# Weight columns interleaved by stage, reversed operands in four stages, and 256 bytes behind the split weight tiles

## The reference, cut to what matters

```python
z = modulate(rmsnorm(x, norm1_g), shift1, scale1) @ w_in + b_in          # stage w_in
x = x + gate1 * (concat(rmsnorm(y_a), rmsnorm(y_b)) @ w_out)             # stage w_out
g_ff, up_ff = split(h2 @ w_ffn_in, 2)                                    # stage ffi0
x = x + gate2 * ((silu(g_ff) * up_ff) @ w_ffn_out)                       # stage ffo0
```

## Time and profile before

| | us |
|---|---|
| median of 2 runs | 1760.57 (1760.45 to 1760.68) |
| profiled execution, first to last instruction | 1757.1 |
| around the span (median less span) | 3.5 |
| PE busy in the span | 1679.6 |
| PEld (weight loads) busy | 1311.8 |
| VectorE busy | 916.1 |
| ScalarE busy | 627.2 |
| GpSimd busy | 225.3 |

### The profile page before, as it was taken

One profiled execution on the slowest core, in us unless ns is written; L12 is line 12 of the kernel. 1 busy time (PEld: TensorE's weight loads), 2 busy tenths in 40 slices (PEclk: granted clock), 3 DMA queues, 4 the chain that ended last, 5 costly groups with the idle time before them and its releaser, 6 DMA issues.

```text
span 1757.1 us, 22185 instructions
## 1 busy us (share of the span) xinstructions
PE 1679.6 (96%) x8263; PEld 1311.8 (75%) x8263; DVE 916.1 (52%) x1376; ACT 627.2 (36%) x946; POOL 225.3 (13%) x204
## 2 busy tenths in 40 slices
PE   1999899999999999999999999999998999999996
PEld 1757688888888867666667788888887688888885
DVE  6765676544334463666667544444336644444223
ACT  1324334222223362554555333333226333333221
POOL 5010106998000030000000000003000000000000
PEclk9999999999999999999998999999999899999998
DMA  7565134454332241111101322233211133333221
GB/s 281 204 200 167 40 110 161 169 181 157 109 107 97 69 117 64 37 37 49 37 25 61 108 96 95 95 100 115 98 57 49 61 98 100 99 96 115 92 80 48
DMA packets 48588, 179.27 MB, mean 102 GB/s; under 512 B 5968, under 2 KB 6640, under 8 KB 48272
## 3 DMA queue, kind: packets, MB, share of 16 engines
q1 hardware_dynamic: 43600, 162.04, 27.5%
q0 software_dynamic: 3776, 14.78, 2.7%
q10 hardware_dynamic: 1152, 1.66, 0.4%
HBM read 173.04 MB, written 2.10 MB: 100 GB/s over the span
## 4 chain that ended last, share of the span: by engine, by line
PE 71%; issue 22%; DVE 5%; DMA 1%; ACT 1%; ACTq 1%; POOL 0%; POOLq 0%; DVEq 0%; SPq 0%
PE bank L383 15%; PE bank L385 14%; PE bank L384 14%; PE bank L1437 3%; PE bank L1439 2%; PE bank L1438 2%; PE bank L1545 2%; PE bank L1501 2%; PE bank L1521 2%; DVE ada_acc L1972 1%; PE bank L1172 1%; PE bank L1174 1%; PE bank L1173 1%; PE bank L454 1%; PE bank L1394 1%
## 5 line engine op out<-in xcount | busy, mean ns | idle before, releaser
L309 DVE TENSOR_TENSOR w_lo<-raw,w_hi 128x1024 fp32r<-128x1024 f32 (+1 forms) x229 | 316.4, 1382 | 575.2 <-ACT w_hi L305 574.9
L305 ACT ACTIVATE w_hi<-raw 128x1024 fp32r<-128x1024 f32 (+1 forms) x229 | 258.0, 1127 | 564.4 <-PE bank L385 482.7
L383 PE MATMUL bank<-h_hi,w_hi 128*128 128x512 f32 x1136 | 448.0, 394 | 0.5 <-DVE w_lo L309 0.5
L385 PE MATMUL bank<-h_hi,w_lo 128*128 128x512 f32 x1136 | 442.2, 389 | 0.0
L384 PE MATMUL bank<-h_lo,w_hi 128*128 128x512 f32 x1136 | 442.2, 389 | 0.0
L383 PEld LDWEIGHTS bank<-h_hi,w_hi 128*128 128x128 f32 x1136 | 213.2, 188 | 50.2 <-issue 5.2
L385 PEld LDWEIGHTS bank<-h_hi,w_lo 128*128 128x128 f32 x1136 | 213.2, 188 | 45.0
L384 PEld LDWEIGHTS bank<-h_lo,w_hi 128*128 128x128 f32 x1136 | 213.3, 188 | 44.6 <-issue 1.7
L383 PE MATMUL bank<-hid_hi,w_hi 128*128 128x512 f32 x528 | 205.6, 389 | 0.0
L384 PE MATMUL bank<-hid_lo,w_hi 128*128 128x512 f32 x528 | 205.4, 389 | 0.0
L385 PE MATMUL bank<-hid_hi,w_lo 128*128 128x512 f32 x528 | 205.4, 389 | 0.0
(11 more groups left out here) (397 smaller groups left out, 2079.5 us busy)
## 6 DMA issues: line engine op xcount, KB each, us to landing
raw<-in_f2i SPq DMA_DIRECT2D x88, 512.0 KB, 3.3
raw<-in_ffi SPq DMA_DIRECT2D x44, 512.0 KB, 3.4
raw<-in_f2o SPq DMA_DIRECT2D x32, 704.0 KB, 4.0
ada_w<-in_ada_w SPq DMA_DIRECT2D x24, 512.0 KB, 4.3
m_out<-in_ada_w POOLq DMA_DIRECT2D x24, 512.0 KB, 3.7
raw<-in_att_w SPq DMA_DIRECT2D x23, 512.0 KB, 3.3
raw<-in_ffo SPq DMA_DIRECT2D x16, 704.0 KB, 4.0
raw<-in_ada_w SPq DMA_DIRECT2D x16, 512.0 KB, 4.9
```

Source lines behind the costliest of these rows:

```text
L305: nc.scalar.activation(WH[par][:, 0:kc * P], RAW[s][:, 0:kc * P], ACT.Copy).then_inc(whi, count)
L309: nc.vector.tensor_tensor(WL[par][:, 0:kc * P], RAW[s][:, 0:kc * P], WH[par][:, 0:kc * P].bitcast(F32), ALU.subtract).then_inc(wlo, count)
L383: pe_.matmul(bank[:, :], w_h, hi[:, k0 + k, :], start=start and k == 0, stop=False)
L385: last = pe_.matmul(bank[:, :], w_l, hi[:, k0 + k, :], start=False, stop=stop and k == kc - 1)
```

## The change

A table `MIX` gives for each stage a number r and a flag. The host stores the weights of each group of r chunks interleaved (`_mixed`): element j of chunk k stands at r * j + k within the group (the last group of a tile may be smaller; with r = 11 and 11 chunks it is one group). On the chip `wcols` takes chunk k as every r-th element from `k % r` on. All matmuls that read split weights, and those that read raw ones in L454 and L1394, use it. Where the flag is set, `turned` reverses the moving operand and the output bank along the 512 tokens, so that each output element is what it was. A tile of 64 float32 per partition (256 bytes) that nobody uses is allocated between w_lo1 and x_res. The splits, the DMAs and the waits are as before.

```diff
+MIX = {"w_in": (4, False), "w_out": (8, True), "ffi0": (2, False), "ffo0": (11, False), "att5": (1, False), "att6": (4, True),
+       "att_out": (2, False), "ffi1": (2, True), "ffo1": (4, True), "ffi2": (4, False), "ffo2": (4, False)}
...
         WL = [sb(f"w_lo{i}", [P, KH * P], F32R) for i in range(2)]
+        sb("behind_weights", [P, 64])
         X = sb("x_res", [P, C, S])
...
+        def wcols(tile, k, name, kc=C):
+
+            r = min(MIX[name][0], kc - k // MIX[name][0] * MIX[name][0])
+            at = k // MIX[name][0] * MIX[name][0] * P
+            return tile[:, at + k % MIX[name][0]:at + r * P:r]
+
+        def turned(ap, name):
+            return ap[:, ::-1] if MIX[name][1] else ap
+
+        def block(name, n, par, kc, hi, lo, k0, bank, start, stop, ready=None, between=None):
 
             pe_ = nc.tensor
+            out = turned(bank[:, :], name)
             pe_.wait_ge(wlo, n + 1)
             for k in range(kc):
                 if ready is not None:
                     pe_.wait_ge(n_lo, ready + k + 1)
-                w_h, w_l = WH[par][:, k * P:(k + 1) * P], WL[par][:, k * P:(k + 1) * P]
-                pe_.matmul(bank[:, :], w_h, hi[:, k0 + k, :], start=start and k == 0, stop=False)
-                pe_.matmul(bank[:, :], w_h, lo[:, k0 + k, :], start=False, stop=False)
-                last = pe_.matmul(bank[:, :], w_l, hi[:, k0 + k, :], start=False, stop=stop and k == kc - 1)
+                w_h, w_l = wcols(WH[par], k, name, kc), wcols(WL[par], k, name, kc)
+                x_h, x_l = turned(hi[:, k0 + k, :], name), turned(lo[:, k0 + k, :], name)
+                pe_.matmul(out, w_h, x_h, start=start and k == 0, stop=False)
+                pe_.matmul(out, w_h, x_l, start=False, stop=False)
+                last = pe_.matmul(out, w_l, x_h, start=False, stop=stop and k == kc - 1)
...
-                        m = pe_.matmul(PS[2][:, 2 * t:2 * t + 2], w[:, k * P:(k + 1) * P], SHL[:, k, :],
+                        m = pe_.matmul(PS[2][:, 2 * t:2 * t + 2], wcols(w, k, name), SHL[:, k, :],
...
+def _mixed(w, name):
+
+    b, p, n = w.shape
+    r, kc = MIX[name][0], n // P
+    full = kc // r * r
+    parts = [w[:, :, :full * P].reshape(b, p, full // r, r, P).transpose(0, 1, 2, 4, 3).reshape(b, p, full * P)]
+    if full < kc:
+        parts.append(w[:, :, full * P:].reshape(b, p, kc - full, P).transpose(0, 1, 3, 2).reshape(b, p, (kc - full) * P))
+    return np.concatenate(parts, axis=2)
```

More of the change, by code:

```diff
@@ L395, in up @@
                 nc.tensor.wait_ge(ev[t % 2], cnt + 2 * g + t // 2)
-                block(n + 4 * g + t, t % 2, C, hi, lo, 0, PS[t % 2], True, True)
+                block(name, n + 4 * g + t, t % 2, C, hi, lo, 0, PS[t % 2], True, True)
             def part(t, w, h_, l_, k):
[L399 to L402, removed]
+                w_h, w_l, out = wcols(WH[w], k, name), wcols(WL[w], k, name), turned(PS[t][:, :], name)
+                x_h, x_l = turned(h_[:, k, :], name), turned(l_[:, k, :], name)
+                pe_.matmul(out, w_h, x_h, start=k == 0, stop=False)
+                pe_.matmul(out, w_h, x_l, start=False, stop=False)
+                return pe_.matmul(out, w_l, x_h, start=False, stop=k == C - 1)
             def shift_sums(t):
@@ L453, in pe_phase_renewed @@
                 for t in range(2):
[L454 removed]
+                    m = pe_.matmul(PS[2 + t][:, :], wcols(RAW[t], k, name), XG[:, k, :], start=k == 0,
                                    stop=k == C - 1)
@@ L1168, in _, with part @@
             ada_sums(1, PS[5], raw_used, 2 * C)
[L1170 to L1174, removed]
+            def part(name, t, k, hi, lo, first, last):
+                w_h, w_l, out = wcols(WH[t], k, name), wcols(WL[t], k, name), turned(PS[t][:, :], name)
+                x_h, x_l = turned(hi, name), turned(lo, name)
+                pe_.matmul(out, w_h, x_h, start=first, stop=False)
+                pe_.matmul(out, w_h, x_l, start=False, stop=False)
+                return pe_.matmul(out, w_l, x_h, start=False, stop=last)
             def first_two():
@@ L1183, in first_two @@
                         k = step - LAG
-                        m = part(1, k, HH[:, k, :], HL[:, k, :], k == 0, k == C - 1)
+                        m = part("w_in", 1, k, HH[:, k, :], HL[:, k, :], k == 0, k == C - 1)
                     if step < C:
@@ L1189, in first_two @@
                         pe_.wait_ge(n_lo, nj["n1"].lo + step + 1)
-                        m0 = part(0, step, HH[:, step, :], HL[:, step, :], step == 0, step == C - 1)
+                        m0 = part("w_in", 0, step, HH[:, step, :], HL[:, step, :], step == 0, step == C - 1)
                         if step == C - 1:
@@ L1199, in out_part @@
                 hi, lo = out_chunk(k)
-                return part(t, k, hi, lo, k == CA, k == CA - 1)
+                return part("w_out", t, k, hi, lo, k == CA, k == CA - 1)
             def out_block(n):
@@ L1298, in _ @@
                 pe_.wait_ge(ev[n % 2], n // 2 + 1)
-                block(n, n % 2, C, HH, HL, 0, PS[n % 2], True, True, None, lambda k: inside(n, k))
+                block("w_in", n, n % 2, C, HH, HL, 0, PS[n % 2], True, True, None, lambda k: inside(n, k))
                 if n in (5, 7, 9):
@@ L1363, in lin @@
                 pe_.wait_ge(ev[t % 2], O0[name] // 2 + 2 * g + t // 2)
-                block(N0[name] + 4 * g + t, t % 2, C, HH, HL, 0, PS[t % 2], True, True, ready, between)
+                block(name, N0[name] + 4 * g + t, t % 2, C, HH, HL, 0, PS[t % 2], True, True, ready, between)
             def att_part(w, low, k):
[L1367 to L1370, removed]
+                w_h, w_l, out = wcols(WH[w], k, "att5"), wcols(WL[w], k, "att5"), turned(PS[w][:, :], "att5")
+                x_h, x_l = turned(HH[:, k, :], "att5"), turned(low[:, k, :], "att5")
+                pe_.matmul(out, w_h, x_h, start=k == 0, stop=False)
+                pe_.matmul(out, w_h, x_l, start=False, stop=False)
+                return pe_.matmul(out, w_l, x_h, start=False, stop=k == C - 1)
             n5, cnt5 = N0["att5"], O0["att5"] // 2
@@ L1383, in _ @@
                 for half, w_ in enumerate((WH[0], WL[0])):
-                    m = pe_.matmul(PS[2][:, 0:2], w_[:, k * P:(k + 1) * P], FSH[:, k, :], start=k == 0 and half == 0,
+                    m = pe_.matmul(PS[2][:, 0:2], wcols(w_, k, "att5"), FSH[:, k, :], start=k == 0 and half == 0,
                                    stop=k == C - 1 and half == 1, skip_group_check=True)
@@ L1393, in _ @@
                 for t in range(2):
-                    m = pe_.matmul(PS[3 + t][:, :], RAW[2 + t][:, k * P:(k + 1) * P], XG[:, k, :], start=k == 0,
+                    m = pe_.matmul(PS[3 + t][:, :], wcols(RAW[2 + t], k, "att5"), XG[:, k, :], start=k == 0,
                                    stop=k == C - 1)
@@ L1400, in _ @@
             pe_.wait_ge(ev[0], cnt5 + 1)
-            block(n5 + 4, 0, C, HH, HL, 0, PS[0], True, True, nj["q0"].lo)
+            block("att5", n5 + 4, 0, C, HH, HL, 0, PS[0], True, True, nj["q0"].lo)
             lin("att5", 1, 1)
@@ L1435, in lin_step @@
                     pe_.wait_ge(wlo, n + 1)
[L1436 to L1439, removed]
+                w_h, w_l, out = wcols(WH[t], k, name), wcols(WL[t], k, name), turned(PS[t][:, :], name)
+                x_h, x_l = turned(hi[:, k, :], name), turned(lo[:, k, :], name)
+                pe_.matmul(out, w_h, x_h, start=first, stop=False)
+                pe_.matmul(out, w_h, x_l, start=False, stop=False)
+                m = pe_.matmul(out, w_l, x_h, start=False, stop=last)
                 if last:
@@ L2571, in _layout @@
             2, 0, 1, 3).reshape(ADA_N * C, P, D),
[L2572 to L2575, removed]
+        "w_in": _mixed(np.concatenate(order), "w_in"), "w_out": _mixed(_blocks(a["w_out"][0]), "w_out"),
+        "ffi": _mixed(gu(f[:CF], f[CF:]), "ffi0"),
+        "ffo": _mixed(_down(a["w_ffn_out"][0]), "ffo0"), "ln_rows": np.stack([a["a_ln_g"][0], a["a_ln_b"][0]]),
+        "ws": a["a_spatial_w"][0].transpose(2, 0, 1), "bs": a["a_spatial_b"][0], "att_w": np.concatenate([_mixed(att[:7], "att5"), _mixed(att[7:], "att6")]),
+        "att_out": _mixed(_blocks(ow), "att_out"), "bf": a["fox_b_f_2"][0].reshape(NH, 1), "pe": a["nsa_cmp_pe_2"][0].transpose(2, 0, 1),
         "w1": a["nsa_cmp_w1_2"][0].reshape(2, CMPB, DH, DH).transpose(2, 0, 1, 3),
         "w2": a["nsa_cmp_w2_2"][0].transpose(1, 0, 2), "pool_w": pw,
-        "f2i": np.concatenate([gu(_blocks(a["ffn_w_gate_2"][i]), _blocks(a["ffn_w_up_2"][i])) for i in range(2)]),
-        "f2o": np.concatenate([_down(a["ffn_w_down_2"][i]) for i in range(2)]),
+        "f2i": np.concatenate([_mixed(gu(_blocks(a["ffn_w_gate_2"][i]), _blocks(a["ffn_w_up_2"][i])), f"ffi{i + 1}")
+                               for i in range(2)]),
+        "f2o": np.concatenate([_mixed(_down(a["ffn_w_down_2"][i]), f"ffo{i + 1}") for i in range(2)]),
     }
```

7 lines of the change are left out of this document (3 added, 4 removed).

## The result

The changed kernel takes 1823.28 us against 1760.57: ratio 1.0358, 95% interval 1.0328 to 1.0388, 62.7 us slower. I had forecast 1771 and a range that ended at 1806. The profiled execution has a span of 1821.6 us, 64.5 more than before.

What follows compares the result with a forecast made beforehand. PE's pace was taken as the bound: 5928 split-weight matmuls at 226.7 ns, 1344 us. Span 1757.1 + 10.5 (interleave; reversal and gap 0) = 1767.6, plus 3.5 around it: 1771 us, +0.6%; range for 8 in 10, 1709 to 1806.

Steps and rivals of the forecast that it cites:

- Part 1: Forecast's term for the interleave, r by stage: +10.5 us, all from loads not hidden; even stretches counted as 0.
- It fits, by some 5 ns: Even stretches, r=4 and more: with the slower load a matmul could start after 221 ns, against 226.7 today.
- my sum: Load of 128 columns at r=4 and more: 213 + 5 = 218 ns, from a halved load pace.
- Rival (b): Slower: halved load becomes PE's bound at r=4 and more, 235 ns a matmul, 1801 us in all; chance 0.15.
- its far end of 250 ns: Rival (b) if matmuls also waited as long again as the load's own start-up: 1854 us.
- also 0: Even stretches of r=2 stages (ffi0, att_out, ffi1; 2256 matmuls): no cost, placed between unit step and L1420's stepped load.
- the paragraph on the earlier trace: Why 10.9 ns a matmul weren't counted as gain: 388 ns without a load beside, 389 with; 65 us at most.
- five slower starts behind a break: Trace before the change: behind a break five matmuls come 0.23 to 0.24 us apart before settling; counted for rival (a), faster, 0.29.
- open loads: Loads not hidden behind small float32 matmuls: att6 80 x 0.107 = 8.6 us, w_in and w_out 1.9 us.
- Part 2: Reversed moving operand and output in w_out, att6, ffi1, ffo1, 2112 matmuls: taken as 0, bounds -23 and +865 us.
- Rival (c): The reversed stream costs: each 10 ns is +21 us, 1792 us at 10 ns; chance 0.07.
- Part 3: The 256 bytes that move every tile behind w_lo against the weights: 0, as h_hi and hid_hi have the same pace.

## Why the prediction was wrong, by its own steps

**The bound and the method were right.** The difference is PE's pace, read by stage from the starts, as the earlier trace rows had it before, and 4.6 us of half clock in w_in that no term of mine had; splits, DMAs and evacuations did not matter.

**Part 1, r=4: the step that failed is "It fits, by some 5 ns", and with it "I take 0 for the even stretches".** The even stretches at r=4 cost 22.1 us in 2832 matmuls, the largest single miss. It failed twice over. The load is longer than my sum: I took 107 ns more from L1420, and in att6, where loads stand alone, a load at r=4 takes 308 ns against 187 to 188, 120 more. It is 13 ns over the sum with 5 to spare, and with a stream of one element the load alone holds the pace at 233.3. And the question was too narrow: I asked only whether the load is hidden. At r=3 it is (215.8 ns with a stream of one element), half a load at r=4 is short (193 ns), and both cost the full stream nearly as much, 235.7 and 232.5 ns. Rival (b) named 235 ns from r=4 on, and 235.0 to 235.2 is what w_in, ffi2 and ffo2 show. Its reason, a load's 213 ns at half pace stretched to 227, fits the 120 ns but is only half of the story, since r=3 pays without it. I gave it 0.15, because 31 columns could not show the 6%; with an estimate that left 5 ns of room I should have given it more.

**Part 1, r of 8 and 11: mis-sized.** I took all r from 4 on as one, since the 128-byte step of L1420 lay beyond them all and seemed to bound them. It does not: r=6 costs about as r=4, but with a stream of one element the pace is 237.7 ns at r=8 and 246.9 at r=11, where it is 233.3 at r=4. w_out and ffo0 cost 18.5 us, where rival (b) had 720 x 8.4 ns = 6.0; only its far end of 250 ns came near.

**Part 1, r=2: "also 0" failed.** That is 15 us in 2256 matmuls, and the same narrow question. The load is hidden as I said (193 ns), and the pace is 233.3 all the same. I put it "between unit step and the L1420 row", which looks only at the load's length and not at what it does to the stream beside it. The argument for that was the paragraph on the earlier trace rows: a stream without a load beside it takes 388 ns and one with takes 389; "so the excess belongs to the full-pace stream". The one-element runs confirm that. What does not follow is that a load can't add to it: that a load in the best of places takes nothing doesn't say that every load does., five slower starts behind a break with the same operands, was a sign that the pace is not fixed by the operands alone, and I priced it only as a possible gain.

**Part 1, open loads: right.** 80 loads at 0.107 us, 8.6 us forecast; the L1455 group has 543 ns where I wrote 530, and 10.6 us by the table. All of att6 took 11.2 us longer, its pace included.

**Part 2: 0 forecast, 6.7 ns a matmul measured alone in the even stretches, and 0 in the change,** but for w_out's 0.7 us, since r of 2 and more already costs as much. (Alone it came to 9.4 us; 2112 x 6.7 ns would be 14, but att6, where other matmuls stand between, lost only 3.5 ns a matmul.) So this step was wrong by itself and did next to no harm to the sum; that was luck. Rival (c) priced 10 ns.

**Part 3: right for 256 bytes,** 1.0005. The reason I gave, that tiles at different places have the same pace, was worth less than I thought: a gap of 256 bytes leaves every place within 64 bytes as it was, and 32 bytes would have been 35 us.

**The page of the Trainium skill** (TensorE: Matmul & The Clock Gate, Part 2) says that loading takes nothing from a running matmul. For float32r at full clock the runs differ: r=2 and a shifted load slow the stream by 4 to 7 ns with the load well hidden. The measurement decides. The Trainium skill's note on cachelines (SBUF — State Buffer, "SBUF: two separate sides") did well for the load's length up to a step of 16 bytes, as far as its two hits in a line go: 193 ns at 8 bytes, 252 at 12, 308 at 16. The same note counts a step of four float32 as free, which the 308 ns against 188 contradict, and has no reason for the 334 and 345 ns at 32 and 44 bytes. It says nothing of the pace of the stream beside the load.

## What to carry to other kernels

A row in which something is free shows that it can be free, not that it always is: where two streams read the same memory, ask what the change does to their places against each other, and price both signs. That a load is hidden doesn't make it free: here loads of 193 and 252 ns, both hidden, cost the stream 7 to 9 ns a matmul. And 5 ns of room on a sum of estimates is no room when 3552 matmuls stand behind it. As far as these runs go, read weights for float32r matmuls at unit step, stream forwards, and keep the split tiles and the activations at the distance that was measured to be good (here none, or 256 bytes; 32 bytes were bad).

## What the runs showed of the hardware

- A float32r matmul of 512 columns follows the last by 226.7 ns, and by 215.8 if its stream reads one element. To the latter a load at a step of 4 or 12 bytes does nothing (215.8 ns with both); at 16, 32 and 44 bytes the load holds it at 233.3, 237.7 and 246.9 ns.
- The time of a load of 128 float32 columns by its step, beside a full stream: 187 to 188 ns at 4 bytes, 193 at 8, 252 at 12, 308 to 310 at 16, 304 to 308 at 24, 331 at 32, 345 at 44. Beside a stream of one element the record is not shorter: 328 ns at 16 bytes, 334 at 32, 345 at 44.
- The pace of a full stream by the step of the load: 226.7 ns at 4 bytes, 233.3 at 8, 234.9 to 235.7 at 12, 235.1 at 16, 236.3 at 24, 244.7 at 32, 254.2 at 44.
- Reading the stream backwards costs 6.7 ns at r=1, nothing more at r=2, takes 1.8 off at r=4 and adds 3.7 at r=8; writing the bank backwards costs nothing.
- Shifting a load by 4 to 60 bytes against the stream costs 0 to 6.7 ns, without order that I can see (0 at 12 and 28 bytes, 3.3 at 16, 6.7 at 56). Many settings end at just 233.3 ns, 6.7 above the 226.7, by different ways (r=2, reversal, r=4 with reversal, r=4 with a stream of one element, a gap of 32 bytes, seven of the fourteen places). I have no account of why these two values; it stays open.
